# Two dot products moved ahead of VectorE's mid-turn addition in the PEER part of a decoder trunk

## The chip, the cores and the metric

The kernel is one program on one core of a Trainium2 chip. The metric is the device time of one execution in microseconds (us); lower is better. The engines are named as in the profile: PE is TensorE (matrix products), PEld its weight load, DVE is VectorE, ACT is ScalarE, POOL is GpSimd (here it issues the gathers), SP is SyncE (it issues the plain loads).

## The reference

A decoder trunk of two layers on 256 tokens of width 2048. Each layer has a mixer (attention, HGRN2 and mLSTM heads side by side between two projections) and then the PEER part, in which the change lies:

```
q  = (xt @ w_query).reshape(t, 8, 2, 128)
s1, s2 = q[:, :, 0] . sub_keys[0], q[:, :, 1] . sub_keys[1]   # 128 scores each
top 16 of each, top 16 of their 256 sums -> idx (16 of 16384 experts), gate = softmax
pre = einsum('td,thkd->thk', xb, expert_u[ib])
act = gelu(pre) * gb
out = einsum('thk,thkd->td', act, expert_v[ib])
x   = x + out
```

So for every token and each of 8 heads, 16 rows of `expert_u` are gathered and dotted with the token's vector, and 16 rows of `expert_v` are gathered and added up with the weights `act`.

## The kernel before, in words

Tokens lie on the 128 partitions in two blocks, b = 0 and 1. A *group* is one head and one block: 16 groups in a layer, and in each group 16 steps k. One step gathers one row per token from a table, 128 rows of 8 KB, 1 MB in all.

- **POOL** (`fetch`, L964 to L981) issues every gather, in one written order. In a loop over the first seven heads (h = 0 to 6) it issues u row k of group (h, 1), then v row k of group (h, 0), for k = 0 to 15; then u row k of (h+1, 0) and v row k of (h, 1). Each kind has a ring of four buffers, `urow` and `vrow` (RING = 4). u row k waits on `u_free` until the dot product k-4 is done; v row k waits on `v_free` until the sum k-4 is done. Since POOL works in order, a v row that has to wait also holds the u rows behind it, and the other way round.
- **DVE** (`dots`, L1443 to L1449) waits for a u row and multiplies it with the normalised tokens `hn`, with the sum going to `pre`. After the 16th dot of a group, `activate` (L1453 to L1456) makes the weights `act_k`, with gelu on ACT.
- **ACT** (`diagonals`, L919 to L929) turns weight k into a 128x128 diagonal matrix in a ring of four, `diag`. A diagonal waits until the sum k-4 is done.
- **PE** (`sum_rows`, L707 to L717) multiplies the diagonal with the v row into four banks of PSUM, 4 matrix products for each k, which stand in the trace as 8 records. The 16 steps of a group add up there.
- **DVE** (`take_sum`, L1458 to L1463) waits until PE has done the group's last sum, adds the four banks to the residual `xs` and signals `sum_taken`. There is only one set of four banks, so PE's first sum of the next group waits for `sum_taken`.

The order in which DVE works is written out by hand. One pass of its loop is a *head turn*. It has a take_sum of the first block, `take_sum(h, 0)`, in its middle, and one of the second block, `take_sum(h, 1)`, at its end. In the middle the order is: dots 8 to 15 of group (h, 1), `activate(h, 1)`, `take_sum(h, 0)`, dots 0 to 5 of group (h+1, 0), and then `choose(h + 1, 1)`, the selection of the top 16 for the next group. There are 7 head turns in each of 2 layers, so 14 such places in an execution. I call this place the *mid-turn*. The last head is written behind the loop and has no such place.

Names in the trace: `work` holds urow and vrow, `work<-in_peer_u_dram` and `work<-in_peer_v_dram` are the two gathers, the DVE instruction on L1449 is a dot product (each is followed by a short read of its accumulator), L1462 is the addition in take_sum, L716 is a sum on PE, L929 a diagonal on ACT.

Of the kernel before, what the change touches and what calls it, by code (L numbers as in the profile page):

```python
# [125 lines left out]
def trunk(nc, x, norm_mix, w_in, w_out, attn_sinks, hgrn_lb_logits, hgrn_out_norm, mlstm_conv, mlstm_i_bias,  # L126
          mlstm_f_bias, norm_ffn, peer_query, peer_sub_keys, peer_u, peer_v, norm_final, consts, out):
    with ExitStack() as ctx:
# [119 lines left out]
        def bank(i, n=1):  # L248
            return PS[:, i:i + n, :].rearrange("p b n -> p (b n)")
# [180 lines left out]
        def _(pe):  # L430
# [31 lines left out]
            def project(l, p):  # L462

                j, q = p // 4, p % 4
                name, _, n = SLABS[j] if j < NS else ("w_out", 0, 512)
                pe.wait_ge(lo_ready.sem, lo_ready.upto(l, p + 1))
                w = [m[:, 0:QC * n].rearrange("p (c n) -> p c n", c=QC).bitcast(F32R) for m in (hi[p % HIS], lo[p % LOS])]
                h = [m[:].bitcast(F32R) for m in hT]
                dst = pair(j)
                for i in range(QC):  # L470
                    c = QC * q + i
                    first, last = c == 0, c == NC - 1
                    if name in ("fh", "qh", "qkm0", "qkm1"):
                        d = dst.rearrange("p b (m t) -> p (b m) t", m=2)
                        for m in range(4):

                            mm = products(d[:, m, :], [x[:, i, m * P:(m + 1) * P] for x in w], [x[:, c, :] for x in h],
                                          first and m % 2 == 0, last and m % 2 == 1)
                    else:
                        for b in range(NB):  # L480
                            mm = products(dst[:, b, 0:n], [x[:, c, b * P:(b + 1) * P] for x in h], [x[:, i, :] for x in w], first, last)
                mm.then_inc(pieces_used.sem, 1)
# [516 lines left out]
        def _(dve):  # L999
# [62 lines left out]
            with dve.Fori(0, DEPTH) as l:  # L1062
# [316 lines left out]
                def split_query(h, s):  # L1379

                    dve.wait_ge(wq_hi_ready.sem, wq_hi_ready.upto(l, 2 * h + s + 1))
                    dve.tensor_tensor(lo[s][:].bitcast(F32R), raw0[:], hi[s][:], ALU.subtract).then_inc(wq_lo_ready.sem, 1)  # L1382
# [57 lines left out]
                def v_indices(h, b):  # L1440
                    dve.tensor_copy(idx_v[b][:], idx_u[b][:]).then_inc(vidx_ready.sem, 1)

                def dots(h, b, ks):  # L1443

                    g = h * NB + b
                    for k in ks:
                        dve.wait_ge(u_loaded[k % RING].sem, ((l * GROUPS + g) * (TOPK // RING) + k // RING) * 16 + 16)
                        r = urow[k % RING]
                        dve.tensor_tensor_reduce(r, r, hn[:, b, :], 1.0, 0.0, ALU.mult, ALU.add, pre[:, b, k:k + 1]  # L1449
                                                 ).then_inc(u_free.sem, 1)  # L1450

                def activate(h, b):

                    dve.drain().then_inc(dotted.sem, 1)
                    dve.wait_ge(gelued.sem, l * GROUPS + h * NB + b + 1)
                    dve.tensor_tensor(act_k[:, b, :], act_k[:, b, :], gate[:, b, :], ALU.mult).then_inc(act_ready.sem, 1)  # L1456

                def take_sum(h, b, last=False):  # L1458


                    dve.wait_ge(v_free.sem, v_free.upto(l, V_SUMS if last else (h * NB + b + 1) * TOPK))
                    dve.tensor_tensor(xs[:, b, :], xs[:, b, :], bank(0, 4), ALU.add)  # L1462
                    dve.drain().then_inc(sum_taken.sem, 1)  # L1463
# [14 lines left out]
                with dve.Fori(0, HEADS - 1) as h:  # L1478

                    dots(h, 1, range(0, 2))  # L1480
                    split_query(h + 1, 0)
                    dots(h, 1, range(2, 4))
                    split_query(h + 1, 1)
                    dots(h, 1, range(4, 8))
                    choose(h + 1, 0)
                    v_indices(h, 1)
                    dots(h, 1, range(8, TOPK))
                    activate(h, 1)
                    take_sum(h, 0)

                    dots(h + 1, 0, range(0, 6))
                    choose(h + 1, 1)
                    v_indices(h + 1, 0)
                    dots(h + 1, 0, range(6, TOPK))
                    activate(h + 1, 0)
                    take_sum(h, 1)
# [35 lines left out]
```

## Time and profile before

| | |
|---|---|
| median of 3 runs | 3951.8 us (3949.55 to 3954.76) |
| span of the profiled execution | 3948.3 us |
| PE busy | 2936.3 us, 74% |
| DVE busy | 2179.7 us, 55% |
| POOL busy | 1373.3 us, 35% |
| ACT busy | 743.2 us, 19% |
| HBM read | 1240.14 MB, 315 GB/s over the span |

The span runs from the first to the last instruction of the one profiled execution. The page gives no other time for that execution; the median of the runs is 3.5 us above its span. No engine is busy all the time, so the share of busy time does not say what bounds the kernel. That is read from the waits, stretch by stretch.

### The profile page before, as it was taken

The numbers are of one execution on the slowest core, as the hardware profiler recorded it, in microseconds if no ns is written. First come the engines' busy times: TensorE is split into PE (matmuls) and PEld (weight loads), VectorE is DVE, ScalarE is ACT, GpSimd is POOL, SyncE is SP. The second block draws the span as 40 slices with busy tenths as digits, with TensorE's granted clock in tenths as the row PEclk, the third lists the DMA queues.
The fourth block names the chain that finished last, engine by engine and source line by source line (L and its number), as shares of the span: only waits on it lengthen the run. The fifth ranks groups of instructions, "written<-read, shape, count | busy, mean of one in ns | idle before, by whom it ended". The sixth has DMA issues, their size and how long they took to land.

```text
span 3948.3 us, 33455 instructions
## 1 busy us (share of the span) xinstructions
PE 2936.3 (74%) x10507; PEld 1709.1 (43%) x10507; DVE 2179.7 (55%) x3060; ACT 743.2 (19%) x1151; POOL 1373.3 (35%) x1028
## 2 busy tenths in 40 slices
PE   7999727677767776767889996377777776867776
PEld 7877613333233333332388775233332323333322
DVE  6665556464655564555366645664655564555653
ACT  4344301111111111110043432011110111111110
POOL 0000054453535444544200000544535454544442
PEclk9999869898989898989989998698989898989999
DMA  5434389999989898989844343899989898989897
GB/s 190 145 117 157 112 350 375 366 380 372 387 340 420 337 422 340 418 332 418 344 140 139 129 155 121 344 385 369 391 344 418 345 422 338 419 341 418 334 421 301
DMA packets 288482, 1243.55 MB, mean 315 GB/s; under 512 B 24632, under 2 KB 98432, under 8 KB 156032
## 3 DMA queue, kind: packets, MB, share of 16 engines
q0 software_dynamic: 147456, 1073.81, 66.8%
q1 hardware_dynamic: 140928, 168.51, 13.4%
q8 instruction: 52, 0.85, 0.1%
q14 instruction: 46, 0.38, 0.0%
HBM read 1240.14 MB, written 2.10 MB: 315 GB/s over the span
## 4 chain that ended last, share of the span: by engine, by line
DMA 36%; PE 28%; DVE 20%; issue 8%; DVEq 3%; ACT 3%; POOL 2%; POOLq 0%; SPq 0%; ACTq 0%
DMA work<-in_peer_v_dram,idx_v 17%; PE PS L459 15%; DMA raw<-in_peer_query_dram 11%; PE PS L716 10%; DMA work<-in_peer_u_dram,idx_u 7%; DVE work L1449 7%; POOL work L978 2%; DVE xs L1462 2%; DVE lo L1382 2%; DVE lo L1073 1%; DVE gain L1393 1%; ACT hi L777 1%; DVE gain L1394 1%; ACT hi L894 1%; DVEq L1164 1%
## 5 line engine op out<-in xcount | busy, mean ns | idle before, releaser
L716 PE MATMUL PS<-work,diag 128*128 128x512 f32 x4032 | 1888.8, 619 | 650.1 <-DMA work<-in_peer_v_dram,idx_v 569.0
L1449 DVE CUSTOM_DVE_ANT_0 work<-work,hn 128x2048 f32<-128x2048 f32 x512 | 1160.7, 2290 | 648.3 <-DMA work<-in_peer_u_dram,idx_u 634.7
L716 PEld LDWEIGHTS PS<-work,diag 128*128 128x128 f32 x4032 | 762.3, 197 | 1745.3 <-issue 1201.2
L978 POOL DMA_INDIRECT work<-in_peer_u_dram,idx_u x512 | 754.7, 1474 | 1805.5 <-issue 619.9
L978 POOL DMA_INDIRECT work<-in_peer_v_dram,idx_v x512 | 618.4, 1208 | 743.1 <-PE PS L716 641.2
L459 PE MATMUL PS<-hT_hi,hi 128*128 128x256 f32 x1024 | 313.4, 306 | 250.3 <-DVE lo L1382 240.0
L929 ACT ACTIVATE diag<-cst,act_k 128x128 f32<-128x128 f32 x504 | 188.2, 396 | 1084.3 <-PE PS L716 1072.1
L459 PEld LDWEIGHTS PS<-hT_hi,hi 128*128 128x128 f32 x1024 | 213.0, 208 | 272.2 <-DVE lo L1382 257.1
L459 PE MATMUL PS<-hT_lo,hi 128*128 128x256 f32 x1024 | 305.1, 298 | 0.0
L459 PE MATMUL PS<-hT_hi,lo 128*128 128x256 f32 x1024 | 304.3, 297 | 0.0
L459 PE MATMUL PS<-hi,hT_hi 128*128 128x512 f32 (+1 forms) x704 | 278.4, 395 | 11.6 <-ACT work L801 4.2
L459 PE MATMUL PS<-lo,hT_hi 128*128 128x512 f32 (+1 forms) x704 | 273.1, 388 | 0.0
L459 PE MATMUL PS<-hi,hT_lo 128*128 128x512 f32 (+1 forms) x704 | 272.8, 388 | 0.0
L1382 DVE TENSOR_TENSOR lo<-raw,hi 128x2048 fp32r<-128x2048 f32 x32 | 73.3, 2289 | 358.9 <-ACT hi L894 358.5
L1073 DVE TENSOR_TENSOR lo<-gain,hi 128x2048 fp32r<-128x2048 f32 (+1 forms) x60 | 133.4, 2223 | 168.4 <-ACT hi L777 89.9
L459 PEld LDWEIGHTS PS<-hT_lo,hi 128*128 128x128 f32 x1024 | 213.2, 208 | 1.8 <-issue 1.7
L459 PEld LDWEIGHTS PS<-hT_hi,lo 128*128 128x128 f32 x1024 | 212.4, 207 | 0.0
L1073 DVE TENSOR_TENSOR lo<-raw,hi 128x2048 fp32r<-128x2048 f32 (+1 forms) x60 | 133.4, 2223 | 119.0 <-PE PS L459 92.7
L459 PEld LDWEIGHTS PS<-hi,hT_hi 128*128 128x128 f32 x704 | 135.5, 193 | 39.9 <-issue 8.9
L894 ACT ACTIVATE hi<-raw 128x2048 fp32r<-128x2048 f32 x32 | 60.9, 1903 | 470.7 <-DMA raw<-in_peer_query_dram 457.2
L459 PEld LDWEIGHTS PS<-hi,hT_lo 128*128 128x128 f32 x704 | 135.6, 193 | 27.1
L459 PEld LDWEIGHTS PS<-lo,hT_hi 128*128 128x128 f32 x704 | 135.6, 193 | 24.9
(220 smaller groups left out, 1626.7 us busy)
## 6 DMA issues: line engine op xcount, KB each, us to landing
raw<-in_w_in_dram SPq DMA_DIRECT2D x40, 1024.0 KB, 5.0
gain<-in_w_in_dram SPq DMA_DIRECT2D x40, 1024.0 KB, 5.0
raw<-in_peer_query_dram SPq DMA_DIRECT2D x32, 1024.0 KB
raw<-in_w_out_dram SPq DMA_DIRECT2D x16, 1024.0 KB, 5.1
gain<-in_w_out_dram SPq DMA_DIRECT2D x16, 1024.0 KB, 5.0
work<-in_peer_u_dram,idx_u POOLq DMA_INDIRECT x512
work<-in_peer_v_dram,idx_v POOLq DMA_INDIRECT x512, 12.6
xs<-in_x_dram SPq DMA_DIRECT2D x1, 2048.0 KB, 9.1
```

What stands on the lines that cost most here:

```text
L459: mm = pe.matmul(dst, left[a], right[b], start=(first and i == 0), stop=(last and i == 2))
L716: mm = pe.matmul(PS[:, j, :], diag[:, k % RING, :], vrow[k % RING][:, j * 512:(j + 1) * 512], start=(k == 0), stop=(k == TOPK - 1))
L777: act.activation(hi[p % HIS][:, 0:n_].bitcast(F32R), raw[p % RAWS][:, 0:n_], ACT.Copy).then_inc(hi_ready.sem, 1)
L894: act.activation(hi[s][:].bitcast(F32R), raw0[:], ACT.Copy).then_inc(wq_hi_ready.sem, 1)
L929: act.activation(diag[:, k % RING, :], ident, ACT.Copy, scale=act_k[:, b, k:k + 1]).then_inc(diag_ready.sem, 1)
L978: pool.indirect_dma_start(out=rows_[k % RING], out_offset=None, in_=tables[kind], in_offset=bass.IndirectOffsetOnAxis(ap=idx[b][:, k:k + 1 ...
L1073: dve.tensor_tensor(lo[p % LOS][:, 0:n_].bitcast(F32R), raw[p % RAWS][:, 0:n_], hi[p % HIS][:, 0:n_], ALU.subtract).then_inc(lo_ready.sem, 1)
L1164: dve.drain().then_inc(level_taken.sem, 1)
L1382: dve.tensor_tensor(lo[s][:].bitcast(F32R), raw0[:], hi[s][:], ALU.subtract).then_inc(wq_lo_ready.sem, 1)
L1393: dve.max_index(idx[:, 0:8], vals[:, 0:8], src)
L1449: dve.tensor_tensor_reduce(r, r, hn[:, b, :], 1.0, 0.0, ALU.mult, ALU.add, pre[:, b, k:k + 1]).then_inc(u_free.sem, 1)
L1462: dve.tensor_tensor(xs[:, b, :], xs[:, b, :], bank(0, 4), ALU.add)
```

## The change

In the middle of a head turn, dots 0 and 1 of group (h+1, 0) are issued before `take_sum(h, 0)`, and dots 2 to 5 after it. Before, all six came after it.

```diff
                     v_indices(h, 1)
                     dots(h, 1, range(8, TOPK))
                     activate(h, 1)
+                    dots(h + 1, 0, range(0, 2))
                     take_sum(h, 0)
 
-                    dots(h + 1, 0, range(0, 6))
+                    dots(h + 1, 0, range(2, 6))
                     choose(h + 1, 1)
                     v_indices(h + 1, 0)
                     dots(h + 1, 0, range(6, TOPK))
```

What stands on DVE at the mid-turn. L1455 and L1456 are activate, L1461 is the wait of take_sum and L1462 its addition; the first L1449 rows are dots 0 and 1 of the next group. The difference, with before as - and changed as +:

```order
 L1455 ISA
 L1456 TENSOR_TENSOR act_k<-act_k,gate 128x16
+L1447 ISA
+L1449 ISA work,pre<-work,hn 128x2048
+L1449 ISA pre 128x1
+L1449 ISA work,pre<-work,hn 128x2048
+L1449 ISA pre 128x1
 L1461 ISA
 L1462 TENSOR_TENSOR xs<-xs,PS 128x2048
```

The two dots, each with its accumulator read, and a wait of `dots` now stand between activate and the wait of take_sum. The other half of the same place on DVE, behind the addition:

```order
 L1462 TENSOR_TENSOR xs<-xs,PS 128x2048
-L1447 ISA
-L1449 ISA work,pre<-work,hn 128x2048
-L1449 ISA pre 128x1
-L1449 ISA work,pre<-work,hn 128x2048
-L1449 ISA pre 128x1
 L1449 ISA work,pre<-work,hn 128x2048
 L1449 ISA pre 128x1
```

The same five rows are gone from behind it; the row that now follows the addition is dot 2. Nothing is added or removed, and on PE, ACT, POOL and SP every instruction keeps its place.

## Rows read from the trace of the kernel before

**Rows 1.** The page: DMA share in 40 slices, and the chain that ended last.
```profile
DMA  5434389999989898989844343899989898989897
DMA 36%; PE 28%; DVE 20%; issue 8%; DVEq 3%; ACT 3%; POOL 2%; POOLq 0%; SPq 0%; ACTq 0%
```

**Rows 2.** Stretches of 41 us from a mid-turn on; columns as named in the first row.
```profile
core 0: us, PE busy (x) PEld busy (x) DVE busy (x) ACT busy (x) POOL busy (x), PEclk, DMA share, GB/s
651.00:692.00 41.00, 29.66 (x65) 11.50 (x64) 28.35 (x56) 4.84 (x12) 13.76 (x13) 1.00 1.01 420
1021.00:1062.00 41.00, 31.50 (x67) 12.24 (x65) 28.53 (x56) 5.00 (x12) 14.73 (x14) 0.96 1.01 422
3719.00:3760.00 41.00, 29.43 (x65) 11.50 (x64) 29.35 (x56) 5.08 (x12) 15.81 (x14) 1.00 1.01 422
```

**Rows 3.** DVE around the mid-turn at 1021.9; in brackets idle time before and its releaser.
```profile
1010.65 2.29 DVE L1449 CUSTOM_DVE_ANT_0 work<-work,hn 128x2048 f32<-128x2048 f32 x1 [3.17 <-DMA work<-in_peer_u_dram,idx_u]
1015.60 2.29 DVE L1449 CUSTOM_DVE_ANT_0 work<-work,hn 128x2048 f32<-128x2048 f32 x1 [2.65 <-DMA work<-in_peer_u_dram,idx_u]
...
1021.90 2.29 DVE L1462 TENSOR_TENSOR xs<-xs,PS 128x2048 f32<-128x2048 f32 x1 [3.50 <-PE PS L716]
1024.44 2.29 DVE L1449 CUSTOM_DVE_ANT_0 work<-work,hn 128x2048 f32<-128x2048 f32 x1 [0.25 <-issue]
1026.66 2.29 DVE L1449 CUSTOM_DVE_ANT_0 work<-work,hn 128x2048 f32<-128x2048 f32 x1
1030.52 2.29 DVE L1449 CUSTOM_DVE_ANT_0 work<-work,hn 128x2048 f32<-128x2048 f32 x1 [1.56 <-DMA work<-in_peer_u_dram,idx_u]
1032.73 0.08 DVE L1449 DVE_READ_ACCUMULATOR2_ANT pre<- 128x1 f32 x1
1035.49 2.29 DVE L1449 CUSTOM_DVE_ANT_0 work<-work,hn 128x2048 f32<-128x2048 f32 x1 [2.68 <-DMA work<-in_peer_u_dram,idx_u]
1037.71 0.08 DVE L1449 DVE_READ_ACCUMULATOR2_ANT pre<- 128x1 f32 x1
1040.46 2.29 DVE L1449 CUSTOM_DVE_ANT_0 work<-work,hn 128x2048 f32<-128x2048 f32 x1 [2.67 <-DMA work<-in_peer_u_dram,idx_u]
```

**Rows 4.** PE around the same mid-turn (x8 is one sum, x24 three).
```profile
1018.19 3.67 PE L716 MATMUL PS<-work,diag 128*128 128x512 f32 x8 [1.29 <-DMA work<-in_peer_v_dram,idx_v]
1024.51 12.28 PE L716 MATMUL PS<-work,diag 128*128 128x512 f32 x24 [2.65 <-DVEq L1463]
1038.09 3.67 PE L716 MATMUL PS<-work,diag 128*128 128x512 f32 x8 [1.30 <-DMA work<-in_peer_v_dram,idx_v]
1042.97 3.70 PE L716 MATMUL PS<-work,diag 128*128 128x512 f32 x8 [1.21 <-DMA work<-in_peer_v_dram,idx_v]
```

**Rows 5.** POOL around the same mid-turn.
```profile
1022.67 0.94 POOL L978 DMA_INDIRECT work<-in_peer_v_dram,idx_v  x1 [2.74 <-PE PS L716]
1027.55 2.21 POOL L978 DMA_INDIRECT work<-in_peer_u_dram,idx_u  x1 [3.94 <-DVE pre L1449]
1030.47 0.94 POOL L978 DMA_INDIRECT work<-in_peer_v_dram,idx_v  x1 [0.71 <-issue]
1031.71 1.90 POOL L978 DMA_INDIRECT work<-in_peer_u_dram,idx_u  x1 [0.30 <-issue]
1033.92 0.94 POOL L978 DMA_INDIRECT work<-in_peer_v_dram,idx_v  x1 [0.30 <-issue]
```

**Rows 6.** ACT there: diagonal 4, released by the first sum's end.
```profile
1029.70 0.40 ACT L929 ACTIVATE diag<-cst,act_k 128x128 f32<-128x128 f32 x1 [7.40 <-PE PS L716]
```

**Rows 7.** A sum after PE had been idle for 6.9 us or more.
```profile
1000.99 6.67 PE L716 MATMUL PS<-work,diag 128*128 128x512 f32 x8 [6.94 <-DMA work<-in_peer_v_dram,idx_v]
2966.75 8.80 PE L716 MATMUL PS<-work,diag 128*128 128x512 f32 x16 [6.86 <-DMA work<-in_peer_v_dram,idx_v]
3700.41 8.71 PE L716 MATMUL PS<-work,diag 128*128 128x512 f32 x16 [8.25 <-DMA work<-in_peer_v_dram,idx_v]
```

**Rows 8.** A gather issued to empty DMA queues, and the dot that waits for it.
```profile
991.37 2.20 POOL L978 DMA_INDIRECT work<-in_peer_u_dram,idx_u  x1 [9.31 <-PE PS L716]
998.12 2.29 DVE L1449 CUSTOM_DVE_ANT_0 work<-work,hn 128x2048 f32<-128x2048 f32 x1 [0.92 <-DMA work<-in_peer_u_dram,idx_u]
```

**Rows 9.** All v gathers, from the start of the issue to the landing.
```profile
DMA to landing us min/median/max: 5.6/12.6/18.0
```

## The prediction

> **What bounds the kernel now.** I read the page first: the DMA engines are 80 to 90% busy in every slice of the PEER part, and DMA is the largest share of the chain that ended last [rows 1]. Then I asked for the stretches of 41 us that begin at each of the 14 mid-turns. In all 14 the DMA share is 1.01 at 420 to 422 GB/s; the first, the third and the last stand in [rows 2]. So from the mid-turn on, for 41 us, the DMA engines never pause. The change acts inside a stretch in which the transfers alone set the pace.
>
> The timeline of DVE shows that pace. Dots that wait for their row start at 1010.65 and 1015.60 before the addition, and at 1030.52, 1035.49 and 1040.46 after it [rows 3]. These are steps of 4.97 us: one u row and one v row, about 2.49 us each. The rows between them by the same step land at 1020.6 (u row 0) and 1025.5 (u row 1); nobody waits for them, since DVE is waiting for PE and then adding. On PE, v row 3 is waited for until 1038.09 and v row 4 until 1042.97 [rows 4], again on that beat. PE starts the first sum of the next group at 1024.51, after 2.65 us of waiting for the addition [rows 4]. POOL waits 3.94 us for dot 0 before it issues u row 4 at 1027.55, then issues v row 4 at 1030.47 and u row 5 at 1031.71 [rows 5].
>
> **What the change moves.** No instruction is added or removed. Two dots go ahead of one addition at 14 places. I work it out at the mid-turn at 1021.9.
>
> *Dot 0* can start when u row 0 lands, 1020.6, instead of 1024.44. It ends at 1022.8. That releases u row 4 on POOL. POOL issues v row 3 at 1022.67 for 0.94 us and then needs 0.30 us more [rows 5], so u row 4 goes out at 1023.9 instead of 1027.55: 3.6 us earlier. What is that worth? The DMA engines are full until its turn comes, and dot 4 waited for it until 1040.46, on the beat. I price this at 0.
>
> *Dot 1* must wait for u row 1, landing 1025.5, and takes 2.2 us to the next start (1024.44 to 1026.66 in [rows 3]). The addition therefore starts at 1027.8 instead of 1021.90, 5.9 us later. It was waiting for PE, now it waits behind a dot that itself waits for a transfer. It ends at 1030.1, before dot 2 may start at 1030.52, so dots 2 to 5 and the selection behind them keep their times.
>
> *PE* waits for `sum_taken`, so its first sum starts 5.9 us later, at 1030.4. PE has then been idle for 8.6 us. What does the first sum cost after such a pause? Before, it takes 5.2 us (1024.51 until ACT is released at 1029.70 [rows 6]). After 6.9 to 8.3 us of idle time I find 6.67 us for one sum, and 8.80 and 8.71 us for two [rows 7]; less 3.65 us for the second, that is 5.1 us each. I take 6.1 us, between the two. The first sum then ends at 1036.5, and between 1035.5 and 1037.1 at the ends.
>
> *v row 4* is issued 0.8 us behind the end of that sum (1029.70 to 1030.47): at 1037.3, instead of 1030.47. This is the point of the whole change: the issue slips by 6.8 us. The row landed at 1042.97, 12.5 us after its issue, because it queued behind others. How late may it go out without being missed? [Rows 8] show a gather into empty queues. It is issued at 991.37 for 2.20 us and its row is there at 998.12, that is 4.55 us from the end of the issue. The shortest time from the start of an issue to the landing is 5.6 us [rows 9], and 0.94 + 4.55 is 5.5. So the last harmless start is about 1042.97 - 5.5 = 1037.5. The margin is 0.2 us: nearly used up, at each mid-turn.
>
> One more thing comes in. POOL's issue takes 0.94 us, but 1.90 or 2.21 when a dot is running as it starts: the issue from 1031.71 ends at 1033.61, 0.88 us behind the end of the dot at 1032.73 [rows 3, 5]. At 1037.3 dot 3 is running, until 1037.71. So the issue ends at 1038.6, not 1038.2, and v row 4 lands at 1038.6 + 4.55 = 1043.15, 0.2 us late. With the slow first sum the issue starts at 1037.9, ends at 1038.8, and the row lands at 1043.4, 0.4 us late. I take 0.3 us.
>
> The Trainium skill (SBUF — State Buffer, "DMA never contends with a compute engine" and the points around it) says that a DVE instruction with two SBUF inputs contends only with a GpSimd instruction that reads SBUF, and that descriptor generation needs the write interface, so it would not be held. A dot has two SBUF inputs, and this trace shows the issue held until 0.88 us behind it, so here the measurement decides. By the page's reading v row 4 would land on its beat and the slip would be nothing.
>
> *Is it paid back or repeated?* Behind v row 4 on POOL stands u row 5: it goes out near 1039, instead of 1031.71, and is needed at 1045.4; harmless. Sums 1, 2 and 3 have their rows and run back to back at 3.65 us, so they end at 1040.2, 1043.8 and 1047.5. v row 5 goes out at 1041.0, in dot 4 (until 1042.7), its issue ends at 1043.6 and it lands at 1048.1; its beat, moved by 0.3, is 1048.2. Each further sum gains 1.3 us on the beat (4.97 - 3.65), so after some seven sums PE is back in its old place. ACT's diagonals follow the sums and have 0.40 us of work each. The gathers that wait behind the selection, 40 us on, do not see it. But the 0.3 us lost by the DMA engines stays lost, since they are the bound to the end of the half turn.
>
> **Sum.** 14 x 0.3 = 4 us on the profiled span of 3948.3, so 3952.5; with the 3.5 us by which the median lies above that span, 3956.0. Against 3951.8 that is 0.1%, less than the 0.2% (7.9 us) that a measurement of this kernel can tell from no change. The bounds: from below 0, if the first sum is always the quick one and no issue is held. From above, v row 4 starts its issue at 1037.9 and takes the full 6.75 us of the empty-queue gather [rows 8] to land, 1044.65, which is 1.7 us late: 14 x 1.7 = 24 us, 3975.
>
> **Rivals.**
> *The queue runs dry (slower).* One mechanism: v row 4 is held back on POOL by the late first sum, and u row 5 behind it, so that for a moment nothing is queued. It costs up to 1.7 us a mid-turn, 3960 to 3975. For it: the margin I find is 0.2 us in an estimate made of three durations, and the issue of both streams hangs on the same wait. Against it: the first sum was quick in two of the three cases in [rows 7], and u row 4 still occupies the engines almost to its own landing. It decides from 0.56 us a mid-turn (7.9 / 14), when v row 4's issue ends after 1039.0. Chance 0.20.
> *The earlier dots pay (faster).* u row 4 goes out 3.6 us earlier, and POOL's wait of 3.94 us for dot 0 [rows 5] goes. If POOL's wait were on the path this would give 14 x 3.6 = 51 us, 3901; if a fifth of it counted, 3942. For it: it is the longest wait of POOL there. Against: the DMA share of 1.01 through the same 5 us, and each row landing on its beat. Chance 0.06.
> *Nothing at all.* The slip is absorbed: 3952. With my forecast it makes the case of no measurable change. The order of DVE does change as the diff says, so a change without effect on the instructions is no rival.
>
> **Chances and range.** My case with the absorbed one, 3950 to 3960: 0.74. Slower by over 0.2%: 0.20. Faster by over 0.2%: 0.06. The range reaches into the slower case until about one in ten is left out above, 3971, and 3946 below for the spread of the runs and a small gain.
>
> **What would show it.** In the profile after: the addition at a mid-turn waits for no engine's sum but starts about 5.9 us after PE's last sum; PE's wait for it grows from 2.65 to 8.5 us; the first sum takes 5.1 to 6.7 us; POOL's wait for dot 0 is gone and a wait of more than 10 us for PE stands before v row 4; that row lands 0 to 0.5 us behind its beat; the DMA share of the 41 us stays at 1.00 or 1.01; the next end of the head turn comes later by the same 0.3 us. I am wrong if the DMA share there falls to 0.98 or less (the slower rival), or if the distance from one mid-turn to the next gets shorter.

## The result, and the profile after

| | before | changed |
|---|---|---|
| median of 5 runs | 3954.76 us (3949.55 to 3956.29) | 3972.32 us (3967.54 to 3979.85) |
| profiled execution: span | 3948.3 us | 3975.6 us |
| its own time | | 3977.47 us |

The ratio is 1.0041, with a 95% interval of 1.0028 to 1.0055. The change makes the kernel slower by 0.41%, some 16 us. That is more than the 0.2% that can be told from no change, so the likeliest case of the prediction (3956, no measurable difference) did not come true, and the slower rival did. The median lies 1.3 us above the range given. Set against the kernel before as it was timed beside it (3954.76 us, not the 3951.8 us that the prediction started from), the upper end of that range is a ratio of 1.0049, and 1.0041 lies inside. The range held the result only because it reached into the slower case; the forecast itself did not. Of the twelve executions of e1 below, two took 4328 and 12633 us and stand outside its ratio.

The same stretch of 41 us from a mid-turn on, in the changed kernel (it is at 1027.9 now), to be read against [rows 2]:

```profile
core 0: us, PE busy (x) PEld busy (x) DVE busy (x) ACT busy (x) POOL busy (x), PEclk, DMA share, GB/s
655.00:696.00 41.00, 27.77 (x60) 11.73 (x60) 26.60 (x54) 4.67 (x11) 17.86 (x13) 0.87 0.98 397
1027.00:1068.00 41.00, 30.20 (x66) 12.69 (x65) 26.89 (x54) 4.68 (x11) 15.74 (x13) 0.88 0.99 408
3745.00:3786.00 41.00, 29.92 (x66) 12.50 (x65) 26.91 (x54) 4.68 (x11) 15.90 (x13) 0.92 0.99 408
```

The DMA engines moved 420 to 422 GB/s there before. Now it is 393 to 413 in the 14 stretches. At 408, (1 - 408/422) x 41 us = 1.4 us of transfers are missing. Summed over the 14 stretches it is 26 us, and the span grew by 27.3 us. (This profiled execution is one of the longer ones; the medians differ by 17.6 us.)

DVE at this mid-turn, against [rows 3]:

```profile
1026.58 2.29 DVE L1449 CUSTOM_DVE_ANT_0 work<-work,hn 128x2048 f32<-128x2048 f32 x1 [2.16 <-DMA work<-in_peer_u_dram,idx_u]
1031.55 2.29 DVE L1449 CUSTOM_DVE_ANT_0 work<-work,hn 128x2048 f32<-128x2048 f32 x1 [2.67 <-DMA work<-in_peer_u_dram,idx_u]
1033.77 2.28 DVE L1462 TENSOR_TENSOR xs<-xs,PS 128x2048 f32<-128x2048 f32 x1
...
1041.49 2.29 DVE L1449 CUSTOM_DVE_ANT_0 work<-work,hn 128x2048 f32<-128x2048 f32 x1 [2.68 <-DMA work<-in_peer_u_dram,idx_u]
1046.43 2.29 DVE L1449 CUSTOM_DVE_ANT_0 work<-work,hn 128x2048 f32<-128x2048 f32 x1 [2.64 <-DMA work<-in_peer_u_dram,idx_u]
1052.65 2.29 DVE L1449 CUSTOM_DVE_ANT_0 work<-work,hn 128x2048 f32<-128x2048 f32 x1 [3.92 <-DMA work<-in_peer_u_dram,idx_u]
```

Dots 0 and 1 stand ahead of the addition, and the addition follows dot 1 without a pause, 5.9 us behind PE's last sum (1027.88). The dots keep their beat of 4.97 us up to dot 4. Dot 5 breaks it: its wait is 3.92 us instead of 2.67, 1.25 us more. This is where most of the time goes, and it shows on row u5, not on row v4 (which lands 0.5 us late).

PE, ACT and POOL there, against [rows 4 to 6]. The last row but one is the stretch of the first sum; its third number from the end is the granted clock:

```profile
1024.21 3.67 PE L716 MATMUL PS<-work,diag 128*128 128x512 f32 x8 [1.30 <-DMA work<-in_peer_v_dram,idx_v]
1036.37 22.85 PE L716 MATMUL PS<-work,diag 128*128 128x512 f32 x48 [8.49 <-DVEq L1463]
...
1036.37:1042.06 5.69, 5.69 (x9) 2.57 (x10) 2.87 (x3) 0.00 (x0) 0.00 (x0) 0.65 1.01 422
...
1042.09 0.40 ACT L929 ACTIVATE diag<-cst,act_k 128x128 f32<-128x128 f32 x1 [13.78 <-PE PS L716]
```

```profile
1029.98 0.93 POOL L978 DMA_INDIRECT work<-in_peer_u_dram,idx_u  x1 [0.30 <-issue]
1042.86 1.73 POOL L978 DMA_INDIRECT work<-in_peer_v_dram,idx_v  x1 [11.95 <-PE PS L716]
1044.90 0.94 POOL L978 DMA_INDIRECT work<-in_peer_u_dram,idx_u  x1 [0.30 <-issue]
```

PE waits 8.49 us for the addition, its first sum ends at 1042.06 (it releases ACT at 1042.09), and six sums, this one among them, run back to back. PE had been idle since 1027.88; the granted clock fell to 0.50 (1.2 GHz) at 1030.16 and was back at 1.00 (2.4 GHz) at 1040.40, so most of the first sum ran at the lower level. POOL issues row u4 at 1029.98 and then has nothing to do for 11.95 us. Row v4's issue starts at 1042.86, while dot 3 runs, and ends at 1044.59, 1.73 us after its start instead of 0.94 us. The DMA engines over the same 5 us, first before (v4 was issued long ago), then in the changed kernel:

```profile
1037.00:1042.00 5.00, 3.67 (x8) 1.44 (x8) 2.33 (x3) 0.43 (x2) 1.93 (x2) 1.00 1.01 421
```

```profile
1043.00:1048.00 5.00, 5.00 (x13) 2.19 (x12) 2.36 (x3) 0.40 (x1) 3.93 (x4) 1.00 0.87 310
...
1044.00:1045.00 1.00, 1.00 (x4) 0.48 (x3) 0.00 (x0) 0.00 (x0) 0.69 (x2) 1.00 0.60 246
1045.00:1046.00 1.00, 1.00 (x4) 0.47 (x3) 0.00 (x0) 0.40 (x1) 0.84 (x1) 1.00 1.06 197
1046.00:1047.00 1.00, 1.00 (x3) 0.38 (x2) 0.57 (x1) 0.00 (x0) 0.70 (x1) 1.00 0.70 270
```

421 GB/s against 310 (share and GB/s are the last two columns): the engines had run out of rows. Note when: from 1044 on, some 2 us before dot 4 sees its row (1046.43). Over the five us (1 - 310/421) x 5 = 1.3 us of transfers are missing, about what row u5 is late. Only half of that is idle time (share 0.87, 0.7 us). The other half lies in the restart: from 1045 to 1046 the share is 1.06 and the rate 197 GB/s. Packets of 8 KB take 0.32 us at most at this place in the kernel before (at two of the 14 mid-turns, two packets take 0.7 us); behind each of the 14 pauses now, 10 to 20 of them take 0.6 to 1.7 us. That is also why a share of 0.98 or less over 41 us, the sign that the prediction named for the slower rival, shows in only 5 of the 14 stretches, while the bytes show the pause in all of them.

### The profile page after: what moved, and what is told of

Same layout as the page of the kernel before. It is cut to its first block, busy times and chain, and to the rows that moved or that the text cites. A ratio compares the mean times of both kernels' runs of the same rounds, so it can differ in the third digit from the quotient of the medians.

```text
span 3975.6 us, 33455 instructions
## 1 busy us (share of the span) xinstructions
PE 2938.7 (74%) x10507; PEld 1720.7 (43%) x10507; DVE 2181.5 (55%) x3060; ACT 742.8 (19%) x1151; POOL 1361.0 (34%) x1028
## 4 chain that ended last, share of the span: by engine, by line
DMA 37%; PE 29%; DVE 16%; issue 8%; DVEq 4%; ACT 3%; POOL 2%; POOLq 0%; SPq 0%; ACTq 0%
PE PS L459 16%; DMA work<-in_peer_v_dram,idx_v 14%; DMA work<-in_peer_u_dram,idx_u 12%; PE PS L716 11%; DMA raw<-in_peer_query_dram 11%; DVE work L1449 5%; POOL work L978 2%; DVE lo L1382 2%; DVEq L1463 1%; DVE lo L1073 1%; DVE xs L1462 1%; DVE gain L1393 1%; ACT hi L894 1%; ACT hi L777 1%; DVE gain L1394 1%
## 5 line engine op out<-in xcount | busy, mean ns | idle before, releaser
L1449 DVE CUSTOM_DVE_ANT_0 work<-work,hn 128x2048 f32<-128x2048 f32 x512 | 1162.4, 2291 | 727.1 <-DMA work<-in_peer_u_dram,idx_u 717.0
L716 PEld LDWEIGHTS PS<-work,diag 128*128 128x128 f32 x4032 | 774.4, 199 | 1767.5 <-issue 1299.0
L978 POOL DMA_INDIRECT work<-in_peer_u_dram,idx_u x512 | 722.5, 1411 | 1750.0 <-issue 628.5
L978 POOL DMA_INDIRECT work<-in_peer_v_dram,idx_v x512 | 638.4, 1247 | 838.2 <-PE PS L716 724.9
```

Of the source, the lines that this page charges most:

```text
L716: mm = pe.matmul(PS[:, j, :], diag[:, k % RING, :], vrow[k % RING][:, j * 512:(j + 1) * 512], start=(k == 0), stop=(k == TOPK - 1))
L978: pool.indirect_dma_start(out=rows_[k % RING], out_offset=None, in_=tables[kind], in_offset=bass.IndirectOffsetOnAxis(ap=idx[b][:, k:k + 1 ...
```

## The experiments

Times in us "behind T" count from the end of PE's last sum before the mid-turn. The loss at a mid-turn is taken from the landings of the rows: by how much v row 8 lands later behind u row 0 than in the undisturbed beat (42.25 us). Each line is from the profiled execution, the ratio from the timed runs. The sums follow the timed losses, but not closely: 23 us against 17.6 us in the changed kernel, 32 against 22.8 in e4, 18 against 15.7 in e11, 87 against 80 in e2.

| kernel | v4 issue starts | it ends | loss at a mid-turn, sum of 14 | ratio (95%) |
|---|---|---|---|---|
| before | 8.2 to 8.9 | 9.1 to 11.8 | 0 in 13 of 14, sum 0.8 | 1 |
| e1 one dot | 8.0 to 11.0 | 9.0 to 11.9 | 0 in 13, sum 0.8 | 1.0000 (0.9990 to 1.0011) |
| e3 changed, PE kept busy | 13.0 to 14.0 | 13.9 to 14.9 | 0 in 13, sum 1.0 | 0.9994 (0.9985 to 1.0004) |
| e9 one product later | 13.6 to 14.1 | 14.6 to 15.0 | 0 in 13, sum 0.5 | 0.9998 (0.9988 to 1.0008) |
| e12 two later, dots 3, 4 cut | 14.5 | 15.7 | 0 to 0.5, sum 2.4 | 1.0004 (0.9993 to 1.0015) |
| e11 two products later | 14.5 | 16.7 | 0.7 to 1.8, sum 18 | 1.0047 (1.0034 to 1.0060) |
| changed | 14.5 to 15.9 | 16.7 to 16.9, once 17.9 | 0.2 to 2.9, sum 23 | 1.0041 (1.0028 to 1.0055) |
| e5 changed, dots 3, 4 cut | 14.4 to 15.4 | 15.6 to 16.4 | 0 to 2.3, sum 16 | 1.0041 (1.0027 to 1.0054) |
| e4 old order, late PE | 13.8 to 15.5 | 14.7 to 16.7 | 0 to 3.2, sum 32 | 1.0050 (1.0038 to 1.0063) |
| e2 three dots | 19.4 to 21.0 | 21.7 to 22.0 | 5.9 to 6.5, sum 87 | 1.0207 (1.0188 to 1.0227) |

In seven of the 14 mid-turns of the kernel before, the issue starts in dot 2 and ends only at 11.7 to 11.8; that is early enough, and the beat is kept. The first mid-turn is off the beat by 0.8 us before the change too (its dot 3 starts at 14.4 instead of 13.6); in the lines with 0 in 13 it is the one left over.

**e1, one dot ahead.**

```diff
-                    dots(h + 1, 0, range(0, 2))
+                    dots(h + 1, 0, range(0, 1))
                     take_sum(h, 0)
-                    dots(h + 1, 0, range(2, 6))
+                    dots(h + 1, 0, range(1, 6))
```

> Only dot 0 stands ahead of the mid-turn addition, dots 1 to 5 behind it. Theory A (the late addition makes PE's first sum late, v row 4 is issued too late and the DMA engines run out of work): dot 0 ends 0.9 us behind PE's last sum, so everything on that path slips by only 0.9 us, v row 4 is issued near 9.5 us behind it, and the time is that of the kernel before, ratio 1.000 (0 to +3 us). Theory B (any dot ahead of the addition costs, through the changed order of u and v rows on POOL): about half of the change's loss, +9 us. Theory C (the earlier dots pay): faster than before by some us.

Measured 3957.27 us against 3955.74, ratio 1.0000. Dot 0 does start earlier and row u4 goes out early (1026.72, 2.1 us behind T, instead of 5.7), and it brings nothing. Row v4's issue slips to 1035.61 here, 11.0 behind T, and costs nothing, with the engines at the full 422 GB/s. Theory B falls, and C too, to within the 0.1% of the interval.

```profile
1026.72 0.94 POOL L978 DMA_INDIRECT work<-in_peer_u_dram,idx_u  x1 [0.31 <-issue]
1035.61 0.94 POOL L978 DMA_INDIRECT work<-in_peer_v_dram,idx_v  x1 [7.95 <-DVE pre L1449]
```

The DMA engines there (share and GB/s are the last two columns):

```profile
1025.00:1066.00 41.00, 32.09 (x65) 13.13 (x66) 28.12 (x58) 4.74 (x12) 16.36 (x14) 0.92 1.01 422
```

**e2, three dots ahead** (`range(0, 3)` ahead of take_sum, `range(3, 6)` behind it).

> Dots 0, 1 and 2 stand ahead of the addition. Row 2 lands 5.0 us behind row 1, so the addition slips by another 5.0 us. Theory A: the DMA engines' margin is already used up, so the whole 5.0 us are lost at each of 14 mid-turns: 70 us on top of the change's 18, near 4040 us, ratio about 1.022. Theory B (a cost for each dot moved): 9 us more, near 3981.

Measured 4035.59 us against 3955.74, ratio 1.0207: 80 us over before. Less the 16 us of the change that is 64 us for the third dot, with 70 expected. PE's wait is 13.48 us and POOL's 17.68 us. Between the changed kernel and e2 the issue of row v4 ends 4.95 us later, and a mid-turn loses 4.6 us more: once the margin is gone, nearly every us of lateness is a us lost.

```profile
1050.24 22.33 PE L716 MATMUL PS<-work,diag 128*128 128x512 f32 x45 [13.48 <-DVEq L1463]
...
1057.50 0.94 POOL L978 DMA_INDIRECT work<-in_peer_v_dram,idx_v  x1 [17.68 <-PE PS L716]
```

The DMA engines there (share and GB/s are the last two columns):

```profile
1037.00:1078.00 41.00, 27.26 (x56) 11.56 (x56) 22.68 (x48) 4.48 (x11) 12.86 (x13) 0.83 0.86 353
```

**e3, the changed kernel with PE kept busy.**

```diff
+                def filler(n):
+                    for _ in range(n):
+                        pe.matmul(PS[:, 6, :], ident, cst[:, 0:512], start=True, stop=True)
...
+                    filler(9)
                     for k in range(TOPK):
                         sum_rows(h, 1, k)
```

> The changed kernel, with 9 unused 128x512 products on PE into a free PSUM bank while it waits for the mid-turn addition (7.7 us of the 8.5 us). They keep the granted clock up, so the first sum should take 3.7 us instead of 5.2 to 6.6. The addition is as late as in the changed kernel. Theory A with the slow first sum as a part of it: v row 4 is issued near 13.0 us behind PE's last sum, before dot 3 starts at 13.6, and the DMA engines don't run out: the time returns to that of before, ratio 1.000 (0 to +4 us). If the lateness of the addition alone does it, or the order of the dots: the loss of the change stays, ratio 1.004.

Measured 3955.61 us, ratio 0.9994: the loss is gone, though the addition is as late as in the changed kernel. In the trace of this mid-turn (T is 1020.1) the 18 records of the unused products end at 1027.8 and PE goes on at 1028.60. Row v4's issue starts at 1033.10, 13.0 behind T, 0.6 us before dot 3 (1033.72), and takes 0.94 us. The engines move 422 GB/s, and the granted clock stays at 1.00.

```profile
1019.94 7.89 PE L709 MATMUL PS<-cst 128*128 128x512 f32 x18
1028.60 5.84 PE L720 MATMUL PS<-work,diag 128*128 128x512 f32 x13 [0.77 <-DVEq L1468]
...
1028.60:1032.30 3.70, 3.70 (x9) 1.79 (x10) 2.30 (x2) 0.00 (x0) 0.00 (x0) 1.00 1.01 421
...
1033.72 2.29 DVE L1454 CUSTOM_DVE_ANT_0 work<-work,hn 128x2048 f32<-128x2048 f32 x1 [2.67 <-DMA work<-in_peer_u_dram,idx_u]
...
1033.10 0.94 POOL L983 DMA_INDIRECT work<-in_peer_v_dram,idx_v  x1 [9.96 <-PE PS L720]
```

The DMA engines there (share and GB/s are the last two columns):

```profile
1020.00:1061.00 41.00, 36.27 (x83) 15.00 (x81) 28.11 (x56) 5.08 (x12) 16.71 (x14) 1.00 1.01 422
```

**e4, the old order with a late first sum** (8 such products between the wait for `sum_taken` and the first sum of the mid-turn, in the kernel before).

> The kernel before with DVE's old order, but PE does 8 unused 128x512 products (about 7 to 8 us) between sum_taken and the first sum of the mid-turn. So the first sum is late, ending near 14.2 us behind the last one, and dots 0 and 1 stand where they stood. Theory A: the same loss as the change, +10 to +20 us, ratio 1.003 to 1.005. If the loss comes from the order of the dots on DVE and not from the late sum: ratio 1.000.

Measured 3978.54 us, ratio 1.0050. Dots 0 and 1 stand where they always stood, and the loss is there. So a late first sum is enough to make the loss; the new order of the dots is not needed for it.

```profile
1025.81 8.79 PE L709 MATMUL PS<-cst 128*128 128x512 f32 x16 [2.41 <-DVEq L1468]
...
1038.84 1.28 POOL L983 DMA_INDIRECT work<-in_peer_v_dram,idx_v  x1 [7.55 <-PE PS L721]
```

**e5 and e6, two dots cut in half, in the changed kernel and in the one before.**

```diff
-                    dots(h + 1, 0, range(2, 6))
+                    dots(h + 1, 0, range(2, 3))
+                    half_dot(h + 1, 0, 3)     # columns 0 to 1023 of 2048
+                    half_dot(h + 1, 0, 4)
+                    dots(h + 1, 0, range(5, 6))
```

> The changed kernel, with dots 3 and 4 behind the mid-turn cut to the first 1024 of 2048 columns (it leaves out the other half of these two products). They end 1.1 us earlier, at 14.8 and 19.7 us behind PE's last sum, so POOL's issue of v rows 4 and 5, which in the changed kernel starts at 14.5 to 15.9 and 18.3 to 19.4, is held less or not at all; the addition and the first sum stay as late. Theory H (dots that run hold POOL's issue, and that is most of what empties the DMA engines): the issue of v row 4 ends at 15.7 to 16.9 instead of 16.7 to 16.9, most of the loss goes, ratio about 1.001 (+2 to +8 us). Theory A alone (the late sum does it, holding costs nothing): ratio 1.004.

> Control: the kernel before with the same two dots cut in half (the other half of these two products is left out). In the kernel before DVE waits for rows there and the DMA engines are full, so both theories expect no change: ratio 1.000.

e6 measured 1.0002 (0.9992 to 1.0011), as expected. e5 measured 1.0041 (1.0027 to 1.0054), the same as the changed kernel: theory H in the form I had written down failed here. The trace says why. The first sum is still slow, so in 11 of 14 mid-turns v4's issue starts only after the halved dot, from 15.0 on, and ends at 15.9 to 16.4, nothing having held it. That is too late by itself. The three that end at 15.6 to 15.7 lose 0.0, 0.0 and 0.6 us. So e5 could not tell whether holding costs anything; for that the first sum must end early enough.

**e9 and e10, e3 with one unused product behind `sum_taken`; e10 with the halved dots too.**

> e3 (the changed kernel with 9 unused products during PE's wait) with one more unused product behind sum_taken, so that the first sum ends 0.85 us later than in e3, which lost nothing. v row 4's issue would start at about 13.9 us behind PE's last sum, 0.3 us after dot 3 has started (13.6), instead of 13.0. Theory H (a running dot holds POOL's issue until 0.9 us behind the dot's end): it ends at 16.7 instead of 14.8, the DMA engines run out, and 0.85 us more on PE bring the loss of the changed kernel back: +10 to +25 us, ratio 1.003 to 1.006. If holding costs nothing: the issue is early enough and the ratio is 1.000.

> e9 with dots 3 and 4 behind the mid-turn cut to 1024 of 2048 columns (it leaves out the other half of these two products), so dot 3 ends at 14.8 us and a held issue of v row 4 ends at 15.7 instead of 16.7. In the profiled execution of e5, mid-turns with an issue that ended at 15.7 lost nothing or 0.6 us. Theory H: most or all of e9's loss goes, ratio 1.000 to 1.001. If e9 lost time for another reason (the later sum itself): it loses the same as e9.

Both inconclusive: 0.9998 and 1.0005 (0.9995 to 1.0015). The issue started 0.01 us behind the start of dot 3 (1031.44 against 1031.43 in the trace of e9) and was not held:

```profile
1031.43 2.33 DVE L1455 CUSTOM_DVE_ANT_0 work<-work,hn 128x2048 f32<-128x2048 f32 x1 [2.67 <-DMA work<-in_peer_u_dram,idx_u]
...
1031.44 0.94 POOL L984 DMA_INDIRECT work<-in_peer_v_dram,idx_v  x1 [10.57 <-PE PS L721]
```

**e11 and e12, the same pair with two unused products.**

> As e9, with two unused products behind sum_taken instead of one. In e9 the issue of v row 4 started at 13.63 us, within 0.02 us of dot 3's start, and was not held. Now it should start at 14.5 us, well inside dot 3 (13.6 to 15.9), and would end at 15.4 if nothing held it. Theory H: it is held until 16.7, the DMA engines run out as in the changed kernel, +10 to +25 us, ratio 1.003 to 1.006. If holding costs nothing: an end at 15.4, ratio 1.000 to 1.001.

> e11 with dots 3 and 4 cut to 1024 of 2048 columns (the other half of these two products is left out). The first sum is as late as in e11, but dot 3 ends at 14.9, so the issue of v row 4 ends at 15.7. Theory H: most of e11's loss goes, ratio 1.000 to 1.0015. If e11's loss comes from the late sum alone: the same ratio as e11.

This pair decides it: 1.0047 with whole dots, 1.0004 with halved ones. PE, addition and start of the issue are alike in both (14.5 behind T at all 14 mid-turns). Only the end of the issue differs (and with it the issue of u row 5 behind it), since dot 3 runs 1.1 us longer in e11. First e11, then e12: v4's issue, u5's issue, and the engines over the five us from 15 behind T.

```profile
1034.63 2.24 POOL L984 DMA_INDIRECT work<-in_peer_v_dram,idx_v  x1 [11.44 <-PE PS L721]
1037.17 0.94 POOL L984 DMA_INDIRECT work<-in_peer_u_dram,idx_u  x1 [0.30 <-issue]
```

The DMA engines there (share and GB/s are the last two columns):

```profile
1035.15:1040.15 5.00, 5.00 (x13) 2.14 (x12) 2.35 (x3) 0.40 (x1) 4.09 (x4) 1.00 0.85 303
```

```profile
1036.47 1.17 POOL L984 DMA_INDIRECT work<-in_peer_v_dram,idx_v  x1 [11.43 <-PE PS L721]
1037.95 0.94 POOL L984 DMA_INDIRECT work<-in_peer_u_dram,idx_u  x1 [0.30 <-issue]
```

The DMA engines there (share and GB/s are the last two columns):

```profile
1036.99:1041.99 5.00, 5.00 (x13) 2.14 (x12) 1.23 (x2) 0.40 (x1) 3.37 (x4) 1.00 0.94 341
```

e12's engines do run short here: at 341 GB/s, 1.0 us of transfers is missing over these five us, and yet this mid-turn loses only 0.2 us (e11's, at 303 GB/s: 1.4 us missing, 1.1 us lost). A short dip in the rate need not reach the landings.

**e7 and e8, trying to win time at the head turn.** The kernel before has places where the engines do stand still. One lies in DVE's 25 us wait for the second query load.

```diff
                     split_query(h + 1, 0)
-                    dots(h, 1, range(2, 4))
+                    dots(h, 1, range(2, 8))
                     split_query(h + 1, 1)
-                    dots(h, 1, range(4, 8))
                     choose(h + 1, 0)
```

> What the study points to: a place where the DMA engines do run dry in the kernel before. At the start of a head turn they move nothing from about 33 to 40 us behind the addition (957 to 963 us of the trace), while DVE waits 25 us for the second query load with dots 4 to 7 behind it and their rows loaded. Here dots 4 to 7 stand ahead of that wait (split_query(h + 1, 1)), in the kernel before's order elsewhere. Theory A's lesson (only what ends an idle stretch of the DMA engines counts): u row 8, v row 8 and u row 9 go out during the wait, up to 3 rows of 2.49 us are won at 14 places, up to 100 us: ratio 0.975 to 0.99. Rival: the same DMA engines carry the query load, which lands that much later, and nothing is won: ratio 1.000.

Measured 4061.72 us, ratio 1.0275 (1.0259 to 1.0291): 105 us slower. Both the gain that I hoped for and the rival, no change, were far off. The query load shares the engines with the gathers. With three more rows in the queues ACT gets it after a wait of 40.14 us. In the kernel before:

```profile
956.55 1.91 ACT L894 ACTIVATE hi<-raw 128x2048 fp32r<-128x2048 f32 x1 [32.65 <-DMA raw<-in_peer_query_dram]
```

That is 7.5 us more, and 14 x 7.5 us is 105 us. The sum that would free the next v row stands on PE behind that query, so behind the load the engines have nothing (16 GB/s, then 109) and POOL waits 33.27 us for PE. The work was moved ahead of a transfer on the path, and what stands behind that transfer came later by it. The engines in e7, during the load and behind it, and then the two rows of ACT and POOL:

```profile
1128.00:1167.00 39.00, 19.14 (x79) 11.18 (x77) 16.47 (x15) 0.00 (x0) 16.64 (x11) 0.81 1.01 404
1167.00:1174.00 7.00, 1.86 (x8) 1.86 (x9) 2.29 (x1) 2.49 (x3) 0.00 (x0) 0.50 0.05 16
1174.00:1188.00 14.00, 14.00 (x67) 9.98 (x66) 0.07 (x1) 2.86 (x5) 2.18 (x3) 0.91 0.39 109
...
1198.00:1206.00 8.00, 6.95 (x17) 2.77 (x15) 7.62 (x11) 1.80 (x4) 3.40 (x2) 1.00 0.29 89
```

And the timeline:

```profile
1167.85 1.91 ACT L894 ACTIVATE hi<-raw 128x2048 fp32r<-128x2048 f32 x1 [40.14 <-DMA raw<-in_peer_query_dram]
...
1184.27 0.94 POOL L978 DMA_INDIRECT work<-in_peer_v_dram,idx_v  x1 [33.27 <-PE PS L716]
```

e8 also moves dots 8 and 9 ahead of `choose(h + 1, 0)`.

> e7 with dots 8 and 9 also moved, ahead of choose(h + 1, 0), where DVE waits 7.4 us for the key scores and the DMA engines later stand still for 6 us (988 to 994). If rows 8 and 9 are there by then, their dots fill that wait and release two more u rows: a further 2 to 5 us at 14 places, ratio 0.96 to 0.98. If they aren't, choose is late by that and it is no better than e7.

Measured 3953.84 us, ratio 0.9993 (0.9980 to 1.0006): no change against before. Neither of the two expectations came true (0.96 to 0.98, or no better than e7). ACT's wait for the query load is as long here as in e7 (38 to 41 us at the 14 places in both), so the longer load by itself is not the loss; e7 has the long pause behind the load and the second pause as well (89 GB/s from 1198 to 1206), and e8 has only the long one. Counted against 422 GB/s, the transfers missing in one head turn are 19.5 us in the kernel before (924 to 1010), 26.6 us in e7 (1118 to 1220) and 19.3 us in e8 (920 to 1008). No version here beats the kernel before. The two pauses of the kernel before:

```profile
957.00:963.00 6.00, 2.17 (x10) 2.17 (x11) 4.51 (x4) 2.04 (x3) 0.00 (x0) 0.50 0.08 23
...
988.00:994.00 6.00, 6.00 (x15) 2.35 (x13) 5.93 (x7) 0.40 (x1) 2.33 (x2) 1.00 0.02 10
```

And e8, where the second is closed:

```profile
964.00:986.00 22.00, 15.87 (x72) 12.04 (x73) 6.71 (x5) 5.35 (x8) 1.87 (x2) 0.74 0.26 72
986.00:994.00 8.00, 8.00 (x21) 3.64 (x20) 6.58 (x31) 0.72 (x4) 3.87 (x5) 1.00 1.01 421
```

## Why the prediction went wrong

**The chain of events was right, almost to the tenth.** Predicted against measured, at one mid-turn and in us behind T: the addition at 5.9 (5.89 to 5.91 at 13 of the 14), the first sum from 8.5 (8.49), its length 5.1 to 6.7 (5.16 to 6.62 in the trace), the start of v4's issue at 15.4 (14.5 to 15.9), its end at 16.7 because dot 3 holds it (16.7 at 12 of the 14, 16.9 and, where the whole beat is 1.2 us later, 17.9). u row 4 went out 3.6 us earlier and was worth 0 (e1). The slower rival was the right mechanism too, with its place and its price of 0.56 to 1.7 us a mid-turn; I gave it 0.20.

**The step that failed is the deadline of row v4.** The prediction took "4.55 us from the end of the issue", from one gather into empty queues [rows 8], and put the last harmless end of the issue 4.55 us ahead of v4's beat, 16.5 behind T. The experiments measure it. On the undisturbed beat, ends up to 14.6 lose nothing (e3, e9), 15.7 loses 0 to 0.5 us (e12, 0.2 us in the mean), 16.7 loses 0.7 to 1.8 us (e11, 1.3 us in the mean), and beyond that lateness is lost nearly one for one (e2). If it is so from the deadline on, both means put the deadline at about 15.5, 5.5 us ahead of the beat; this is an estimate, and the runs bound it only to between 14.6 and 15.7. I was too generous by some 1.0 us, and the term of my sum that was mis-sized is the 0.3 us lost at a mid-turn: by this deadline it is 1.3 us, which is also e11's mean. 14 x 1.3 = 18 us, and the medians differ by 17.6 us. That the two meet so closely is partly luck, since the trace of the changed kernel loses 23 us, with the second miss below in it. The 5.6 us of [rows 9], which I took for a confirmation, are the shortest of the 128 gathers into one of the four v buffers, not of all 512.

**Why it failed.** I judged the loss by when row v4 itself would land. It landed 0.2 to 1.8 us late, at this mid-turn 0.5, so that part of the working was nearly right. But a row that meets empty engines lands sooner after its issue (v4: 4.8 us from the end of its issue here, 11.5 us before), and this hides their pause; the row behind it shows what the engines lost, and u5 landed 1.2 us late here. "u row 5 ... goes out near 1039, and is needed at 1045.4; harmless" was one wrong sentence, and "u row 4 still occupies the engines almost to its own landing" was the other. The engines' rate drops some 2 us before the last row is seen to have landed (1044 against 1046.43), so the queue was empty sooner than the beat of landings says.

**A second, smaller miss** is v row 5. In 6 of the 14 mid-turns its issue started within dot 4 as I had foreseen, but with the engines already behind it emptied them once more. These six lost 1.7 to 2.9 us each. Of the other eight, six lost 1.2 or 1.3 us, the first mid-turn 2.1 and one 0.2. In that one mid-turn (T = 1396.3) all issues are at the same times and the engines pause too. The trace shows where it differs: each row ends with 16 packets of 4 bytes, and it lands about 0.4 us behind the last of them. Those of u5 stand within 0.5 us there (22.9 to 23.4 behind T), but spread over 1.4 us (23.0 to 24.4) at the mid-turn shown above. So much of the loss is that some of the 16 came late out of the restart. Why they did not this once stays open.

**Holding.** e11 and e12 show that a running dot holds POOL's issue of a gather and that this costs 0.43% when the margin is thin. The reading of the Trainium skill that I weighed (SBUF — State Buffer, "Who interferes with whom", where the part on descriptor generation is marked as inferred), by which it would not be held, does not fit: 0.94 us when nothing runs, 2.24 us in e11. In the changed kernel itself the hold alone does not decide, since with the slow first sum the issue is late also without it (e5, 1.0041).

**The chances.** The margin that I found was 0.2 us, in an estimate made of three durations, one of them from another situation. On one side of it lay nothing, and on the other a loss at a full us for each us. With a margin that thin the slower case should have had near half of the chance, not a fifth.

## What to carry to other kernels

When transfers set the pace, a step off the path is free only up to the moment at which it delays the next issue past the point where the queues run empty. Look for that point in the bytes moved in each us, not in a lone transfer's latency: busy share hides the slow restart, and a short dip may still cost nothing (e12). Look for the loss on the second row behind the pause. A wait moved behind an operation that itself waits for a transfer can cost a whole beat of that transfer (the addition came 5.9 us later here, and 5.0 us more in e2), and one dot fewer (e1) or an engine kept at its clock (e3) is enough to be back on the safe side. Filling a pause of the DMA engines won nothing where the rows that filled it stood in front of the transfer that ends the pause (e7, e8).

## What the runs showed of the hardware that I had not expected

- A gather's issue that starts 0.01 us behind the start of a dot is not held (e9: 0.94 us), one that starts 0.9 us into it is held to 0.9 us behind its end (e11: 2.24 us). The trace of the kernel before has 438 issues that start while a dot runs. Three start within 0.04 us of the dot's start and take 0.94 us; all others, from 0.07 us on, end 0.88 to 0.90 us behind the dot's end, and the longest takes 3.03 us.
- Nine unused products (7.9 us) in a wait of 8.5 us brought the first sum behind it down from 5.2 to 6.6 us to 3.7 us, granted clock 1.00 over the whole stretch of 41 us (2.4 GHz) instead of 0.88 (1.2 GHz from 1030.16 to 1040.40, 2.4 GHz for the rest). By the release of one buffer this was worth 0.4% of the whole kernel, though PE is not the bound.
- Behind a pause of the DMA engines the first packets are slow: 10 to 20 of them take 0.6 to 1.7 us instead of 0.32 us, and this costs about as much as the pause itself (0.7 us idle, 1.3 us of transfers missing at the mid-turn shown). Why they are slow was not tested.
